# Four weight sums of the down projection: from VectorE in the feed-forward loop to accumulating transfers in memory

## What is computed

```
za, zu, zv, zq, zg = jnp.split(h @ w_in[l], SPLITS, axis=-1)
ya, yb, yc = s5_branch(za), sgu_branch(zu, zv), cross_attention(zq, mem)
gates = jax.nn.sigmoid(zg + b_gate[l]).reshape(bsz, seq, N_BRANCHES, D_MODEL)
merged = gates[:, :, 0] * ya + gates[:, :, 1] * yb + gates[:, :, 2] * yc
x = x + merged @ w_out[l]
hf = _rms(x, g_ffn[l])
x = x + (jax.nn.silu(hf @ w_gate[l]) * (hf @ w_up[l])) @ w_down[l]
return _rms(x, g_final)
```

## Time and profile before

| | us |
|---|---|
| median of 3 runs | 769.4 |
| span of the profiled execution | 768.0 |
| around the span (769.4 - 768.0) | 1.4 |
| PE busy | 759.7 (99%) |
| DVE busy | 550.8 (72%) |
| ACT busy | 355.4 (46%) |
| POOL busy | 315.5 (41%) |

### The profile page before, as it was taken

How to read it: one execution, slowest core, us unless ns; L and a number is a source line. 1 busy time by engine, 2 the same in 40 slices (tenths; PEclk the granted TensorE clock), 3 DMA queues, 4 the chain that set the end, 5 groups by cost and what they waited for, 6 DMA issues and landing times.

```text
span 768.0 us, 9764 instructions
## 1 busy us (share of the span) xinstructions
PE 759.7 (99%) x3562; PEld 629.0 (82%) x3562; DVE 550.8 (72%) x752; ACT 355.4 (46%) x529; POOL 315.5 (41%) x169
## 2 busy tenths in 40 slices
PE   8999999999999999999999999999999999999997
PEld 7788887788888888888888888888888888788886
DVE  6999997684848484246767777777777767746687
ACT  6896567644545433634343433332222323434554
POOL 4456655233333333444443444453545344840000
PEclk9999999999999999999999999999999999999999
DMA  8743333122222343232233886666656567768853
GB/s 271 298 150 130 117 96 114 33 88 82 83 83 76 123 143 99 83 101 91 83 110 110 273 297 223 231 206 203 213 180 211 179 204 237 283 193 252 296 202 126
DMA packets 42371, 126.17 MB, mean 164 GB/s; under 512 B 4192, under 2 KB 6368, under 8 KB 40544
## 3 DMA queue, kind: packets, MB, share of 16 engines
q1 hardware_dynamic: 42192, 125.45, 49.1%
q10 hardware_dynamic: 144, 0.26, 0.1%
HBM read 107.08 MB, written 18.61 MB: 164 GB/s over the span
## 4 chain that ended last, share of the span: by engine, by line
PE 89%; ACT 3%; DVE 3%; POOL 2%; DMA 1%; issue 1%; SPq 0%; ACTq 0%
PE bank L1633 24%; PE bank L1635 24%; PE bank L1634 24%; PE bank L1997 3%; PE bank L1999 3%; PE bank L1998 3%; ACT uc L649 1%; DVE s5p L1007 1%; POOL w_lo L579 1%; PE bank L1874 1%; PE bank L1749 1%; PE bank L1766 1%; DMA xT<-xt_dram 1%; ACT w_hi L589 1%; POOL lo_c L579 1%
## 5 line engine op out<-in xcount | busy, mean ns | idle before, releaser
L528 POOL TENSOR_TENSOR w_lo<-raw,w_hi 128x1024 fp32r<-128x1024 f32 x90 | 218.8, 2431 | 300.1 <-ACT w_hi L589 300.1
L589 ACT ACTIVATE w_hi<-raw 128x1024 fp32r<-128x1024 f32 x112 | 118.8, 1060 | 310.9 <-PE bank L1635 306.3
L1633 PE MATMUL bank<-h_hi,w_hi 128*128 128x512 f32 x608 | 238.5, 392 | 0.3 <-POOL w_lo L533 0.3
L1635 PE MATMUL bank<-h_hi,w_lo 128*128 128x512 f32 x608 | 236.6, 389 | 0.0
L1634 PE MATMUL bank<-h_lo,w_hi 128*128 128x512 f32 x608 | 236.6, 389 | 0.0
L1633 PEld LDWEIGHTS bank<-h_hi,w_hi 128*128 128x128 f32 x608 | 114.2, 188 | 24.6 <-issue 1.0
L1634 PEld LDWEIGHTS bank<-h_lo,w_hi 128*128 128x128 f32 x608 | 114.2, 188 | 23.8 <-issue 0.5
L1635 PEld LDWEIGHTS bank<-h_hi,w_lo 128*128 128x128 f32 x608 | 114.1, 188 | 23.6
L533 POOL TENSOR_TENSOR w_lo<-raw,w_hi 128x512 fp32r<-128x512 f32 x48 | 67.2, 1420 | 52.6 <-ACT w_hi L589 45.8
L1007 DVE TENSOR_TENSOR mix<-mix 128x512 f32<-128x512 f32 x44 | 44.9, 1020 | 13.3 <-DMA mix<-w_dram 12.1
L1007 DVE TENSOR_TENSOR lo<-raw,hi 128x1536 fp32r<-128x1536 f32 (+1 forms) x19 | 33.0, 1742 | 24.2 <-ACT hi L917 24.1
(11 more groups left out here) (319 smaller groups left out, 1398.0 us busy)
## 6 DMA issues: line engine op xcount, KB each, us to landing
raw<-w_dram SPq DMA_DIRECT2D x112, 512.0 KB, 3.4
mix<-w_dram SPq DMA_DIRECT2D x11, 1024.0 KB, 8.0
mix_dram<-mix SPq DMA_DIRECT2D x11, 1024.0 KB, 6.4
raw<-w_dram SPq DMA_DIRECT2D x30, 256.0 KB, 4.1
raw<-mix_dram SPq DMA_DIRECT2D x26, 256.0 KB, 4.0
half_dram<-odd SPq DMA_DIRECT2D x11, 256.0 KB, 8.2
second<-half_dram SPq DMA_DIRECT2D x3, 768.0 KB, 6.0
raw<-mix_dram SPq DMA_DIRECT2D x3, 768.0 KB, 4.3
```

Source lines behind the costliest of these rows:

```text
L528: nc.gpsimd.tensor_tensor(w_lo[:, s, :], raw[:, s, :], fv(w_hi[:, s, :]), ALU.subtract).then_inc(w_ready, 1)
L589: nc.scalar.activation(w_hi[:, slot, :], raw[:, slot, :], ACT.Copy).then_inc(w_rounded, 1)
L1633: mm(out, a[0], b[0], start=first, stop=False)
L1635: return mm(out, a[1], b[0], start=False, stop=last)
```

## The change

The sums are made in memory, and the sign of some of them changes so that only additions remain (b11+b12, b12+b22, b11+b12+b22, and b21 plus the last). It has four parts.

1. SP copies each w_down tile from `w_dram` to `mix_dram`, memory to memory, 512 KB at a time: 22 copies, one behind the load of each of the tiles 24 to 45.
2. POOL issues 33 accumulating transfers within `mix_dram`: for each pair one that adds b11 to b12 and b12 to b22 (512 KB), one (`add_t2`) and one (`add_t4`) of 256 KB. They stand behind `low_weights` of the even tiles 28 to 56. POOL's list is written out to tile 69 for that, and the loop covers 70 to 113. Every accumulating transfer waits for its predecessors.
3. DVE's four operations per iteration, the loads and stores of `mix` (11 of each, 1 MB) and the waits on them are gone.
4. `s_1` to `s_4` are made with changed signs, two of them by `scalar_tensor_tensor` in place of `tensor_tensor`, and the half products that come in with the other sign are subtracted where they were added. The semaphore `dt_ready` is folded into `trig_ready`.

```diff
@@ SP
             for t in range(8, T_WO):
                 next_weights(t)
+                if 0 <= t - T_J1 < 2 * PAIRS:
+                    copy_pair(*divmod(t - T_J1, 2))
...
+            def copy_pair(i, j):
+                if i:
+                    sp.wait_ge(mix_copied, 32 * i)
+                sp.dma_start(mix_d[i, :, j * TILE:(j + 1) * TILE], w_d[T_DN + 2 * i + j, :, :]
+                             ).then_inc(mix_copied, 16)
...
-                if i == 0 and j == 3:
-                    sp.wait_ge(x1_ready, 5)
-                    load_pair(0)
-                if i > 0 and j == 2:
-                    store_mix(i - 1)
                 if i > 0 and j == 3:
-                    sp.wait_ge(mix_stored, 16 * i)
-                    load_pair(i)
                     store_half(i - 1)
...
-                sp.wait_ge(mix_stored, 16 * (k + 1))
...
+            sp.wait_ge(mix_t4, 16 * PAIRS)
             for k in range(3):
                 load_unit(k)
-            store_mix(PAIRS - 1)
@@ POOL
-            with nc.gpsimd.Fori(T_J1 // NS + 1, T_DN // NS) as i:
+            def add_first(i):
+                pool.wait_ge(mix_copied, 32 * (i + 1))
+                if i:
+                    pool.wait_ge(mix_b11_b12, 16 * i)
+                nc.gpsimd.dma_start(mix_d[i].rearrange("p (a b n) -> p a b n", a=2, b=2)[:, :, 1, :],
+                                    w_d[T_DN + 2 * i].rearrange("p (a n) -> p a n", a=2),
+                                    accum_op=ALU.add).then_inc(mix_b11_b12, 16)
+            def add_t2(i):
+                pool.wait_ge(mix_b11_b12, 16 * (i + 1))
+                if i:
+                    pool.wait_ge(mix_t2, 16 * i)
+                nc.gpsimd.dma_start(mix_d[i, :, 0:WB], mix_d[i, :, 3 * WB:4 * WB],
+                                    accum_op=ALU.add).then_inc(mix_t2, 16)
+            def add_t4(i):
+                pool.wait_ge(mix_t2, 16 * (i + 1))
+                if i:
+                    pool.wait_ge(mix_t4, 16 * i)
+                nc.gpsimd.dma_start(mix_d[i, :, 2 * WB:3 * WB], mix_d[i, :, 0:WB],
+                                    accum_op=ALU.add).then_inc(mix_t4, 16)
+            for t in range(T_J1 + NS, T_FF):
+                low_weights(t % NS, t)
+                for form, late in ((add_first, 4), (add_t2, 8), (add_t4, 12)):
+                    i, odd_tile = divmod(t - T_J1 - late, 2)
+                    if not odd_tile and 0 <= i < PAIRS:
+                        form(i)
+            with nc.gpsimd.Fori(T_FF // NS, T_DN // NS) as i:
@@ ACT
-            act.wait_ge(mix_stored, 16 * PAIRS)
@@ DVE
-                dve.wait_ge(mix_loaded, 16 * i + 16)
-                tt(b22, b22, b12, ALU.subtract).then_inc(mixed, 1)
-                dve.wait_ge(mixed, 4 * i + 1)
-                tt(b12, b12, b11, ALU.subtract).then_inc(mixed, 1)
...
-                tt(s_1, a21, a22, ALU.add).then_inc(ff_sum, 1)
+                tt(s_1, a22, a21, ALU.subtract).then_inc(ff_sum, 1)
...
-                tt(s_4, a12, s_2, ALU.subtract).then_inc(ff_sum, 1)
+                V.scalar_tensor_tensor(s_4, a12, -1.0, s_2, ALU.mult, ALU.subtract).then_inc(ff_sum, 1)
...
-            go(tt(x1_two(2, 1), x1_two(2, 1), s5[:, :, :], ALU.add))
+            go(tt(x1_two(2, 1), x1_two(2, 1), s5[:, :, :], ALU.subtract))
```

More of the change, by code:

```diff
@@ L209, in build @@
         silu = at("silu", o_e + 4096, [P, 2, T])
-        mix = at("mix", o_e + 8192, [P, 4, WB])
         zg = at("zg", o_e, [P, 4, T])
@@ L282, in build @@
         pt_done, pt_act, pt_dve, pv_done, o_hi_s, o_lo_s = sems("pt_done pt_act pt_dve pv_done o_hi_s o_lo_s")
-        dt_ready, ang_ready, trig_ready = sems("dt_ready ang_ready trig_ready")
+        ang_ready, trig_ready = sems("ang_ready trig_ready")
         j1_g, j1_th, j1_merge = sems("j1_g j1_th j1_merge")
@@ L295, in build @@
         ff_g, ff_u, ff_silu, ff_act, ff_sum, ff_hi, ff_lo = sems("ff_g ff_u ff_silu ff_act ff_sum ff_hi ff_lo")
-        mix_loaded, mixed, mix_stored, half_stored = sems("mix_loaded mixed mix_stored half_stored")
+        mix_copied, mix_b11_b12, mix_t2, mix_t4, half_stored = sems(
+            "mix_copied mix_b11_b12 mix_t2 mix_t4 half_stored")
         unit_loaded = [sem(f"unit_loaded{i}") for i in range(7)]
@@ L402, in _ @@
                         load_x(i)
[L403 to L410, removed]
             def store_half(i):
@@ L454, in load_unit @@
                     sp.wait_ge(w_used, T_DN)
-                elif k == 6:
-                    sp.wait_ge(mix_stored, 16 * PAIRS)
                 elif k > 6:
                     unit_split(sp, {7: 0, 8: 1, 9: 2, 10: 6}[k])
-                sp.wait_ge(mix_stored, 16 * (k + 1))
                 slot, done = unit_raw[UNIT_SLOT[k]], unit_loaded[UNIT_SLOT[k]]
@@ L616, in _ @@
             act.wait_ge(vec_loaded, 16)
-            nc.scalar.activation(s5p[:, 0, :], small[:, C_LDT:C_LDT + 16], ACT.Exp).then_inc(dt_ready, 1)
+            nc.scalar.activation(s5p[:, 0, :], small[:, C_LDT:C_LDT + 16], ACT.Exp).then_inc(trig_ready, 1)
             for k in range(4):
@@ L1019, in _ @@
             dve.wait_ge(vec_loaded, 16)
-            dve.wait_ge(dt_ready, 1)
+            dve.wait_ge(trig_ready, 1)
             go(tt(XR, are, DT, ALU.mult))
@@ L1040, in _ @@
                 low_x(k)
-            dve.wait_ge(trig_ready, 1)
+            dve.wait_ge(trig_ready, 2)
             go(tt(ARE, MAG, CS, ALU.mult))
@@ L1464, in _ @@
             a22, a12 = odd[:, 0:HALF], odd[:, HALF:T]
-            b11, b12, b21, b22 = (mix[:, j, :] for j in range(4))
             with nc.vector.Fori(0, PAIRS) as i:
@@ L1488, in _ @@
                 dve.wait_ge(ff_act, 2 * i + 2)
-                tt(s_1, a21, a22, ALU.add).then_inc(ff_sum, 1)
+                tt(s_1, a22, a21, ALU.subtract).then_inc(ff_sum, 1)
                 tt(s_3, a11, a21, ALU.subtract).then_inc(ff_sum, 1)
                 dve.wait_ge(ff_sum, 4 * i + 1)
-                tt(s_2, s_1, a11, ALU.subtract).then_inc(ff_sum, 1)
+                V.scalar_tensor_tensor(s_2, s_1, -1.0, a11, ALU.mult, ALU.subtract).then_inc(ff_sum, 1)
                 dve.wait_ge(ff_sum, 4 * i + 3)
-                tt(s_4, a12, s_2, ALU.subtract).then_inc(ff_sum, 1)
+                V.scalar_tensor_tensor(s_4, a12, -1.0, s_2, ALU.mult, ALU.subtract).then_inc(ff_sum, 1)
                 dve.wait_ge(ff_hi, 2 * i + 1)
@@ L1524, in _ @@
             dve.wait_ge(s5_ready, 2)
-            go(tt(x1_two(2, 1), x1_two(2, 1), s5[:, :, :], ALU.add))
+            go(tt(x1_two(2, 1), x1_two(2, 1), s5[:, :, :], ALU.subtract))
             low_three(3)
-            go(tt(x1_two(0, 1), x1_two(0, 1), s5[:, :, :], ALU.add))
+            go(tt(x1_two(0, 1), x1_two(0, 1), s5[:, :, :], ALU.subtract))
             low_three(4)
@@ L1547, in _ @@
             low_three(13)
-            go(tt(x1_two(2, 1), x1_two(2, 1), u2[:, :, :], ALU.add))
+            go(tt(x1_two(2, 1), x1_two(2, 1), u2[:, :, :], ALU.subtract))
             low_three(14)
@@ L1551, in _ @@
             for j in range(2):
-                tt(x1_at(2 + j, 1), bank[6 + j][:, :], x1_at(2 + j, 1), ALU.add).then_inc(c_ready, 1)
+                tt(x1_at(2 + j, 1), x1_at(2 + j, 1), bank[6 + j][:, :], ALU.subtract).then_inc(c_ready, 1)
             for j in range(2):
-                tt(x1_at(j, 1), x1_at(j, 1), u3[:, j, :], ALU.add).then_inc(c_ready, 1)
+                tt(x1_at(j, 1), x1_at(j, 1), u3[:, j, :], ALU.subtract).then_inc(c_ready, 1)
             low_three(15)
```

## The result

The changed kernel takes 776.6 us (median of 4 runs, 775.75 to 778.41) against 769.55 us before. The ratio is 1.0094, with a 95% interval of 1.0082 to 1.0106: **slower by 0.9%**, some 7 us. No change was forecast, so the forecast was wrong.

What follows compares the result with a forecast made beforehand. The prediction took PE (TensorE), busy for 759.7 of 768.0 us, as the bound; every term came to 0 (DVE's relief -0.24 to 0), so 768.0 + 1.4 = 769.4 us, no change, with a range of 768.6 to 776.

Steps and rivals of the forecast that it cites:

- What goes: Feed-forward loop: dropping DVE's 44 sums (44.9 us busy) and the `mix` transfers returns 0 us, bounds 0 and -0.24.
- Signs, folded semaphore, waits: Sign changes in `s_2` and `s_4`, at most 9 us of DVE, the folded semaphore and removed store waits: 0 us.
- 33 issues on POOL: In the rounds, issues of some 1.0 us each fit POOL's slack ahead of odd tiles: 0 us.
- The first rival: An issue holds POOL over 2.2 us, delaying PE at tiles 41, 47, 53: 772.3 to 789.6 us, chance 0.15.
- Traffic: In the rounds, copies and accumulations raise DMA demand to 344 of 378 GB/s; it fits, closely: 0 us.
- Doubled by sharing it is 6.8 us and still in time.: Tile 50's weight load of 3.4 us, doubled by shared DMA engines, still lands within the 7.3 us available.
- The waits in the lists: SP's waits for copies and POOL's for accumulations (two or four tiles, 11 us or more, after issue): 0 us.
- The demand: DMA traffic in the rounds, accumulations counted twice: 95 + 83 + 166 = 344 GB/s against 378 for all 16 engines.
- The second rival: Accumulations dearer than 2.4 times overfill DMA in the rounds: 777.6 us at three times, 791 at four; chance 0.16.

Runs made afterwards that it cites:

- dve_alone: The kernel before the change with DVE's 44 sums left out and nothing else changed: 770.29 us, ratio 1.0009.
- x_late: The changed kernel with the six loads of xT issued behind tile 57 instead of tile 46: 769.92 us against 769.95, ratio 1.0002.
- small_adds: The changed kernel with its 33 accumulating transfers cut from 512 to 32 columns, number, places and waits kept: 769.88 us, ratio 1.0001.

## Why the prediction was wrong, point by point

- **What goes: 0 us. Right.** PE is busy for 229.00 of 229.00 us in the loop before and after, and dve_alone finds no gain. DVE's busy time fell by more than the 44.9 us of rows 5. The rest is in one row: `parts<-parts,silu` took 26.0 us for 11 before and takes 8.0 now. Before, it mostly started 0.4 us into a pass of POOL and ended with the pass, 2.5 us for one; now it starts 0.3 us ahead of the pass and takes 0.7. That is worth nothing either.

```profile
L1028 DVE TENSOR_TENSOR parts<-parts,silu 128x512 f32<-128x512 f32 x11 | 8.0, 725 | 1.9 <-ACT silu L903 0.7
```

- **Signs, folded semaphore, waits: 0 us. Right**, as far as x_late, which has them all, equals the kernel before. The new `scalar_tensor_tensor` took 411 and 425 ns in the mean (`s_2` and `s_4`), like the `tensor_tensor` it replaces.
- **33 issues on POOL: 0 us. Right.** Taken at 1.0 us each, they are listed with 0.8 to 1.4 us and overlap in a row: 2.55 us for three against the 6.5 us at hand. The first rival (POOL held) is out: small_adds has the same issues at no cost.
- **Traffic: 0 us. This is the step that failed**, and within it one sentence: "Doubled by sharing it is 6.8 us and still in time." It failed twice. The doubling was too small: six of the seven loads of tiles 39 to 45, with no burst in front of them, took 8.2 to 12.8 us, 2.4 to 3.8 times the 3.4 us. PE waited for none of them. And the sentence took the load of tile 50 for all loads of weights. The loads of xT, 2 MB behind tile 46, stood in the order listing of SP in front of tile 47's load, and were not counted as queued ahead of it. Tile 47's load had more time than tile 50's: it went out at 271.85 us before, and ACT rounded it at 282.65, so 10.8 us. Sent out at 274.40 us it had 10.2 (16.6 less the 6.4 that PE lost). It needed 16.6.
- **The waits in the lists were sized by landings without this traffic.** The copies were given 3 us behind the next tile, the accumulations less than the 11 us of two tiles. Copies took up to 13.0 us and held SP for 20.5 us in ten waits; accumulations took up to 14.5 us and held POOL for 7.9. Both stayed in idle time, so these terms came out at 0 with less to spare than was worked out.
- **The demand was nearly right.** 344 of 378 GB/s, a share of 0.91, was worked out; 0.95 was measured. An accumulation was counted twice; by the queues it costs 2.2 times: q0 moves 11.54 MB in 9.8% of 776.7 us (76 us, 152 GB/s), q1 113.92 MB in 44.7% (347 us, 328 GB/s). "It fits, closely" was true of the mean, as x_late shows. The mean was the wrong thing to ask, since the stage contains a burst.
- **The second rival ("the transfers don't fit", 0.16) had the cause, not the mechanism.** It needed an accumulation dearer than 2.4 times and spread its loss over five pairs of tiles. It came at 2.2 times, at one tile, and not by POOL's waits for accumulations (7.9 us, all in its idle time). One sign that it named did come: landings of `raw` over 7 us, in the rounds, well before PE waited. That its 777.6 us lies near the measured time is chance.
- **The price of a wait.** The wait was 6.4 us, and 1.7 us of half clock came on top. The prediction had no term for the clock, since it had no wait.

## What to carry to other kernels

When a change fills a shared resource, check the latest single transfer, not the mean: list what stands ahead of each load in its queue, and take the time that the largest burst leaves. Work moved to where engines have slack is free only until a burst meets it; moving or cutting up the burst can cost nothing, and here undid all of the loss. Relief of an engine that TensorE doesn't wait for is worth nothing, however many microseconds it is, if TensorE is busy for the whole stage.

## What the runs showed of the hardware

- An accumulating transfer from memory to memory took the DMA engines 2.2 times as long per byte written as the other traffic moved took per byte (152 against 328 GB/s), and landed in 9.7 us (512 KB) or 10.6 us (256 KB) in the median, most of them at a share of 0.95.
- Its issue took POOL 0.8 to 1.4 us as listed, or 2.55 us for three in a row, for 32 columns as for 512.
- On full engines, a load of 512 KB behind 2 MB of loads in the same queue landed in 16.6 us; the one just ahead of them in 4.9 us. SP's six issues of those 2 MB took 6.38 us in place of 2.95.
- Without SP's 20.5 us of waits for the copies the kernel was 3.4 to 3.8 us slower; by which mechanism is open.
- TensorE, after idling for 6.4 us, went on at 1.2 GHz for 3.8 us.
